# Four plain columns ahead of the spreading columns, and a later transpose of the last picks

## The reference, cut to what matters

```python
q = (xt @ w_query).reshape(t, 8, 2, 128)
sc = einsum('thpd,hpnd->thpn', q, sub_keys)
s1, i1 = top_k(sc[:, :, 0], 16); s2, i2 = top_k(sc[:, :, 1], 16)
cand = s1[..., :, None] + s2[..., None, :]
top_s, ci = top_k(cand, 16)              # 8 heads x 16 = 128 picked experts a token
gate = softmax(top_s)
act = gelu(einsum('thkd,td->thk', u_tab[experts], xb))
y = einsum('thk,thkd->td', gate * act, v_tab[experts])
```

## Time and profile before

| what | value |
|---|---|
| median of 3 runs | 2949.99 us (2949.53 to 10154.99) |
| the profiled execution | 2946.5 us |
| its span | 2944.7 us |
| TensorE busy | 2789.5 us, 95% of the span |
| VectorE / GpSimd / ScalarE busy | 2153.7 / 1643.1 / 1107.9 us |
| mean rate of the DMA engines | 223 GB/s |
| the stage with the change, from the first to the last unit | about 762 to 1873 us of the span |

### The profile page before, as it was taken

One profiled execution on the slowest core, in us unless ns is written; L12 is line 12 of the kernel. 1 busy time (PEld: TensorE's weight loads), 2 busy tenths in 40 slices (PEclk: granted clock), 3 DMA queues, 4 the chain that ended last, 5 costly groups with the idle time before them and its releaser, 6 DMA issues. The chain is left out here.

```text
span 2944.7 us, 47007 instructions
## 1 busy us (share of the span) xinstructions
PE 2789.5 (95%) x15784; PEld 1525.5 (52%) x15880; DVE 2153.7 (73%) x4204; ACT 1107.9 (38%) x1502; POOL 1643.1 (56%) x1555
## 2 busy tenths in 40 slices
PE   6998899999999999989999999699999999999998
PEld 3444764455566666656666655344444444444443
DVE  3898965211677999989999963567676777777777
ACT  4353434222344444457666753221122222112212
POOL 1333422011233444457666766687777888888884
PEclk9999998999999999999999999899999999999999
DMA  3231021011244555568888889698988999999995
GB/s 121 75 131 38 1 76 76 36 43 36 92 151 144 180 197 189 189 220 308 313 322 316 310 306 318 206 322 324 333 311 303 341 346 334 336 349 344 332 356 213
DMA packets 265183, 657.87 MB, mean 223 GB/s; under 512 B 17520, under 2 KB 116080, under 8 KB 261888
## 3 DMA queue, kind: packets, MB, share of 16 engines
q1 hardware_dynamic: 190928, 387.24, 36.6%
q0 software_dynamic: 74160, 269.52, 25.0%
HBM read 547.11 MB, written 110.10 MB: 223 GB/s over the span
## 5 line engine op out<-in xcount | busy, mean ns | idle before, releaser
L92 POOL TENSOR_TENSOR w_low<-w_ring,w_high 128x1024 f16<-128x1024 f32 x164 | 370.7, 2261 | 896.4 <-ACT w_ring L87 896.3
L1444 PE MATMUL psum<-region_y,w_high 128*128 128x384 f16 x2048 | 668.4, 326 | 8.3 <-POOL w_low L92 6.0
L1446 PE MATMUL psum<-region_y,w_low 128*128 128x384 f16 x2048 | 668.3, 326 | 0.0
L1445 PE MATMUL psum<-region_y,w_high 128*128 128x384 f16 x2048 | 668.3, 326 | 0.0
L1926 PE MATMUL psum<-scores,wh 128*128 128x512 bf16 x1504 | 571.9, 380 | 32.1 <-POOL wl L1974 17.1
L1927 PE MATMUL psum<-vl,wh 128*128 128x512 bf16 x1504 | 572.0, 380 | 25.8 <-POOL wl L1974 24.0
L1928 PE MATMUL psum<-scores,wl 128*128 128x512 bf16 x1504 | 571.6, 380 | 1.7
L1945 ACT ACTIVATE scores<-w_ring 128x1024 bf16<-128x1024 f32 x128 | 135.2, 1056 | 781.2 <-DMA w_ring<-in_v_t_dram 781.2
L2087 DVE TENSOR_TENSOR region_x<-region_x,psum 128x1024 f32<-128x1024 f32 x192 | 233.9, 1218 | 171.6 <-PE psum L1928 168.3
L1969 POOL TENSOR_TENSOR vl<-w_ring,scores 128x1024 bf16<-128x1024 f32 x128 | 275.4, 2152 | 80.4 <-ACT scores L1945 79.0
L1497 ACT ACTIVATE ge<-psum 128x384 f32<-128x384 f32 x256 | 124.8, 488 | 413.5 <-PE psum L1446 411.5
(11 more groups left out here) (260 smaller groups left out, 4783.8 us busy)
## 6 DMA issues: line engine op xcount, KB each, us to landing
w_ring<-in_u_t_dram SPq DMA_DIRECT2D x128, 512.0 KB, 6.1
w_ring<-in_v_t_dram SPq DMA_DIRECT2D x128, 512.0 KB, 5.4
acts_dram<-ge SPq DMA_DIRECT2D x128, 384.0 KB, 4.8
gates_dram<-scores SPq DMA_DIRECT2D x24, 2048.0 KB, 9.4
scores<-gates_dram SPq DMA_DIRECT2D x30, 1536.0 KB, 13.3
scores<-acts_dram SPq DMA_DIRECT2D x30, 1536.0 KB, 20.7
w_ring<-in_w_stream_dram SPq DMA_DIRECT2D x20, 512.0 KB, 3.5
w_ring<-in_w_q_dram SPq DMA_DIRECT2D x16, 512.0 KB, 3.5
```

Of the source, the lines that this page charges most:

```text
L92: pool.tensor_tensor(self.wl[:, s, :], self.wf[:, s, :], self.wh[:, s, :], ALU.subtract).then_inc(self.w_lo, 1)
L1444: pe.matmul(a, uh[:, par, row], xh[:, n, cols], start=(n == 0), stop=False)
L1445: pe.matmul(a, uh[:, par, row], xl[:, n, cols], start=False, stop=False)
L1446: last = pe.matmul(a, ul[:, par, row], xh[:, n, cols], start=False, stop=(n == KC - 1))
```

## The change

Four of the 16 columns alone move ahead of the spreading columns (`LEAD`), and 12 are left. The transpose of the last picks moves from the end of the 64 columns to behind the second of the four; ScalarE's copy of them moves the same way. VectorE takes groups 0 to 3 ahead of its first one-hot set, not one after each pair of sets, and then takes group 4n + j + 4 where it took 4n + j. GpSimd's gathers stay in the same columns.

```diff
+    LEAD = 4
-    ALONE = NK - PICKED - SPREAD
+    ALONE = NK - PICKED - LEAD - SPREAD
-    FIRST_G = PICKED
+    FIRST_G = PICKED + LEAD
+    LAST_G = FIRST_G + SPREAD
-    SWITCH = (FIRST_TILE - AHEAD) // LOOP
+    SWITCH = (FIRST_TILE - AHEAD - LEAD) // LOOP
...
         if between is not None:
             between()
+        for j in range(LEAD):
+            lead(PICKED + j, j % 2, j)
         for j in range(LOOP):
-            spread(PICKED + j, j % 2, 0, j)
+            spread(FIRST_G + j, j % 2, 0, j)
...
-            slots(sp, pick, spread, unroll=alone)
+            slots(sp, pick, lambda s, par, j: pick(s, par, None, j), spread, unroll=alone)
...
-            slots(pe, pick, spread, lambda: turn_selection(TB))
+            def lead(s, par, j):
+                pick(s, par, None, j)
+                if j == 1:
+                    turn_selection(TB)
+
+            slots(pe, pick, lead, spread)
...
-            slots(act, pick, spread, lambda: keep_selection(TB))
+            def lead(s, par, j):
+                pick(s, par, None, lead_half(j))
+                if j == 1:
+                    keep_selection(TB)
+
+            slots(act, pick, lead, spread)
...
             def spread(s, par, n, j, tile=0):
-                gather_next(LOOP * n + (j + 2), (j + 2) % RING, tile)
+                gather_next(LOOP * n + (j + LEAD + 2), (j + 2) % RING, tile)
                 ring.low(pool, par, s + 2)
...
-            slots(pool, pick, spread, load_iota, few=few, last=last)
+            def lead(s, par, j):
+                gather_next(j + 2, (j + 2) % RING, 0)
+                ring.low(pool, par, s + 2)
+
+            slots(pool, pick, lead, spread, load_iota, few=few, last=last)
...
                     octet(n, 2 * j)
                     octet(n, 2 * j + 1)
-                    take_next(LOOP * n + j, j, n, tile)
+                    take_next(LOOP * n + (j + LEAD), j, n + 1, tile)
+
+            for j in range(LEAD):
+                take_next(j, j, 0, 0)
             turn(0, 0)
...
-            with dve.Fori(SPREAD // RING, (NK - PICKED) // RING) as n:
+            with dve.Fori((LEAD + SPREAD) // RING, (NK - PICKED) // RING) as n:
```

More of the change, by code:

```diff
@@ L1270, in select_and_activate @@
     SPREAD = TD // OCT // 2
-    ALONE = NK - PICKED - SPREAD
+    LEAD = 4
+    ALONE = NK - PICKED - LEAD - SPREAD
     LOOP = 4
-    FIRST_G = PICKED
-    assert ALONE > 0 and ALONE % LOOP == 0 and SPREAD % LOOP == 0
+    FIRST_G = PICKED + LEAD
+    LAST_G = FIRST_G + SPREAD
+    assert ALONE > 0 and ALONE % LOOP == 0 and LEAD == LOOP and SPREAD % LOOP == 0
     uh, ul, u_hi, u_lo = ring.wh, ring.wl, ring.w_hi, ring.w_lo
@@ L1347, in select_and_activate, with slots @@
     EXP_IN = 19
-    def slots(eng, pick, spread, between=None, unroll=None, few=None, last=None):
+    def slots(eng, pick, lead, spread, between=None, unroll=None, few=None, last=None):
         for j in range(PICK):
@@ L1360, in slots @@
             between()
+        for j in range(LEAD):
+            lead(PICKED + j, j % 2, j)
         for j in range(LOOP):
-            spread(PICKED + j, j % 2, 0, j)
+            spread(FIRST_G + j, j % 2, 0, j)
         with eng.Fori(1, SPREAD // LOOP if last is None else SWITCH - 1) as n:
             for j in range(LOOP):
-                spread(LOOP * n + (PICKED + j), j % 2, n, j)
+                spread(LOOP * n + (FIRST_G + j), j % 2, n, j)
         if last is not None:
@@ L1369, in slots @@
             for j in range(LOOP):
-                (spread if j < LOOP - 2 else last)(LOOP * n + (PICKED + j), j % 2, n, j)
+                (spread if j < LOOP - 2 else last)(LOOP * n + (FIRST_G + j), j % 2, n, j)
             with eng.Fori(SWITCH, SPREAD // LOOP) as n:
                 for j in range(LOOP):
-                    last(LOOP * n + (PICKED + j), j % 2, n, j)
+                    last(LOOP * n + (FIRST_G + j), j % 2, n, j)
         if unroll is not None:
             for j in range(ALONE):
-                unroll(PICKED + SPREAD + j, j % 2, j)
+                unroll(LAST_G + j, j % 2, j)
             return
@@ L1379, in slots, with lead_half @@
             for j in range(LOOP):
-                pick(LOOP * n + (PICKED + SPREAD + j), j % 2, None, 2 * n + j // 2, j)
+                pick(LOOP * n + (LAST_G + j), j % 2, None, 2 * n + j // 2, j)
         for j in range(LOOP):
             pick(NK - LOOP + j, j % 2, None, (ALONE - LOOP + j) // 2, j)
+    def lead_half(j):
+        return (PICKED - LAST_G) // 2 + j // 2
     def half_pick(n, j):
-        return j + (PICKED + SPREAD) // 2 if n is None else (PICK // 2) * n + j // 2
+        return j + LAST_G // 2 if n is None else (PICK // 2) * n + j // 2
     def half_spread(n, j):
-        return (LOOP // 2) * n + (PICKED // 2 + j // 2)
+        return (LOOP // 2) * n + (FIRST_G // 2 + j // 2)
     def more(s):
```

## The result

The changed kernel takes 2921.38 us as the median of 6 runs, against 2949.76 for the kernel before on the same chip: ratio 0.9915, 95% interval 0.9894 to 0.9935. The ratio is taken over the fast executions alone, so one execution of the kernel before, at 10154.99 us, does not enter it; it is not the quotient of the two medians, which lie 28 us apart. The profiled execution took 2926.67 us, its span is 2924.9.

The account below looks back on a forecast made before the run. TensorE sets the pace, losing 12.6 us at one standstill for VectorE's first one-hot set. 12.6 - 2.2 (first set late) - 0.7 (slip) = 9.7 us gained, 2950.0 - 9.7 = 2940.3 us; range 2933 to 2948.

Parts of the forecast that it names:

- The standstill is removed: TensorE's wait for VectorE's first one-hot set, filled by four plain columns: 10.92 + 1.67 = 12.6 us gained at most.
- GpSimd's queue ahead of column 66: GpSimd's gathers and low part of column 66 end at 1281.7, TensorE wants them at 1280.0: a wait of 1.7 us.
- The low part of 68 is covered by 2 us: GpSimd's low part of column 68 comes at 1295.8 with slow values, wanted at 1297.3: no wait.
- full clock from column 63 on: Sign in the profile after: TensorE's granted clock stays at full from column 63 on.
- The takes: VectorE's four takes ahead of its first set need 14.4 us (10.0 to 18.4); set ready at 1301.7, loss 2.2 us.
- The chain named in the prediction: VectorE's kept picks, preparation, four takes and first set end at 1301.7, later than TensorE's 1301.2, so they set the loss.
- The slip in the spreading columns, 0.7 us: At the spreading columns' start VectorE's reserve is near nothing, so a slip costs TensorE 0 to 1.5 us, 0.7 taken.
- The waits of the columns alone stay: TensorE's waits for low parts of `u`, 6.0 us, belong to the first ten columns alone and stay.
- The end of the stage costs nothing: Last piece issued 26.9 us ahead of the step to `combine`, landing in 8.0 us: no cost, covered by about 19 us.
- the later stretches keep their lengths and move forward: After the removed standstill, if nothing else waits, all 12.6 us are gained and later stretches only start earlier.
- the rivals: All gained, 2937.4 us (0.13); VectorE bound, 2945.1 (0.14); slower from stage end, 2958.9 (0.05); wait only moves, 2950 (0.05).

Follow-up runs that it names:

- e14: The change, with TensorE's last four columns alone as a loop turn, so its program has the length of before: 2939.24 us, ratio 0.9960.
- e17: The change with the gate matrix 24 KB further in HBM: 2926.29 us, ratio 0.9929 to the kernel before.
- e5: The kernel before, first four columns alone written out on TensorE alone (192 matmuls more), order unchanged: 2932.15 us, ratio 0.9939.
- e10: The kernel before with 192 needless matmuls behind TensorE's last group of `combine`: 2935.11 us, ratio 0.9942.
- e13: The kernel before with the gate matrix 24 KB further in HBM, all programs the same: 2934.09 us, ratio 0.9951.
- e3: The change with the transposes and their copies back at the end of the 64 columns: 2923.66 us, ratio 0.9926 to the kernel before.

## Why the prediction was wrong, step by step

- **The standstill is removed: right.** The forecast for the stage was 9.7 us. The pair of profiles gives 12.0; the 15 kernels of the old order are at 1105.1 us on average (1101.0 to 1108.6), those of the new order with the late transpose and no added stall (the change, e14, e17) at 1096.0 (1094.6 to 1098.9): 9.1 us. e14's ratio gives 12 (5 to 19).
- **GpSimd's queue ahead of column 66: right, and partly by luck.** 1281.7 + 1.8 = 1283.5 forecast, 1283.5 measured, a wait of 1.8 where 1.7 was expected. But two terms were off and cancelled: the low part of 65 took 2.91 us and not 2.13, beside a take of VectorE, and the three groups took 3.0 us each, not 3.4. The 3.4 us were read from a group during which VectorE had begun its preparation (1274.36); the group ahead of it, with VectorE at rest throughout, took 3.04. In e14 the wait is 1.1 us and in e17 3.7, in the same order.
- **The low part of 68 is covered by 2 us: wrong by a size.** It came 1.0 us late, as VectorE's preparation took 1289.7 - 1285.2 = 4.5 us and not 2.4, one pass being 3.40 us beside GpSimd. Here e14 waited 2.1 us, with the clock at 0.62 after it; the forecast of full clock from column 63 on held in the change's profile and not in e14's or e17's.
- **The takes: nearly right.** 1289.72 to 1302.65 is 12.9 us for the four (14.4 taken), one pass of them 3.81 us. The first set was due at 1301.7 + 1.8 = 1303.5 and came at 1305.1, so 3.9 us were lost there and not 2.2: the kept picks were 0.9 us late, the preparation 2.1, and the takes gave 1.5 back. The chain named in the prediction set it.
- **The slip in the spreading columns, 0.7 us: not seen.** From the first set to the columns alone the change and e14 have no wait above 0.3 us, e17 one of 1.1.
- **The waits of the columns alone stay: too high in this pair.** They are 2.8 us in place of 6.0, which is most of the 12.0 - 9.7. The other traces say that this is mainly scatter: the waits above 0.3 us there add up to 2.7 to 6.0 us in the 15 kernels of the old order, 4.1 on average, with before the highest, and to 2.5 to 3.7 in the three of the new.
- **The end of the stage costs nothing: right.** From the last Gelu to the first 512-column matmul it is 24.0 us before and 23.6 after.
- **The step that failed** is in the part on the removed standstill: "the later stretches keep their lengths and move forward". The prediction prices the new order and puts the longer program that comes with it at nothing. With TensorE's program longer by 192 matmuls and the order as before, the kernel is 18 us (e5) and 17 us (e10) faster, and `combine` is 18 and 15 us shorter with the same work. With the new order and the old length (e14) `combine` stays long and the gain is 12 us, near the forecast 9.7. None of the rivals had it.

What stays open: no address is seen in these traces, so that a longer TensorE program shifts the gate matrix is inferred (e10, e13, e17), not shown. It is also not shown why 24 KB suit it better, or why 96 matmuls or GpSimd's 384 memsets do nothing.

## What to carry to other kernels

Where a stage waits for a chain that starts late, work that doesn't need the chain can be put in front of it, and the sum can be made from the chain's own rows. A change of under 2% should be tried against a twin that only has its program length (e10, e14) and one that only moves a large HBM tensor (e13), or an accident of length or placement is booked as the idea's gain. Here it was about half of it: the order gave some 12 of the 25 us.

## What the runs showed that I had not expected

A shift of one intermediate tensor by 24 KB in HBM was worth 0.5% (e13, 0.9930 to 0.9971), as much as the standstill. And moving a step earlier, off the path, gained nothing (e3), as VectorE then worked beside GpSimd. What that can cost is seen in the change's own trace: three passes of VectorE with two inputs took 3.14, 3.40 and 3.81 us in place of 1.23, each beside a low part of GpSimd of 2.13 to 2.91 us. This agrees with the rule of the Trainium skill, GPSIMD Engine Reference, Key points, that GpSimd shares its SBUF interfaces with VectorE and contends with VectorE instructions that have two SBUF inputs. No kernel that was run beats the change beyond the intervals.
